# Hymba encoder layer on one core: the first group's last rows are multiplied on GpSimd and scaled on ScalarE instead of normed on VectorE

## The reference

```python
def rmsnorm(x, g):
    xf = x.astype(jnp.float32)
    y = xf * lax.rsqrt(jnp.mean(xf * xf, axis=-1, keepdims=True) + NORM_EPS)
    return (y * g.astype(jnp.float32)).astype(x.dtype)
...
    gu = jnp.einsum('bsd,dn->bsn', rmsnorm(x, ln_ffn_g), w_gate_up)
    g, up = gu[..., :D_FF], gu[..., D_FF:]
    return x + jnp.einsum('bsf,fd->bsd', jax.nn.silu(g) * up, w_down)
...
    return rmsnorm(x, final_norm_g)
```

## Time and profile before

| | |
|---|---|
| runs | 1387.62 us median of 3 (1386.29, 1387.62, 1387.71) |
| profiled execution | span of its instructions 1386.6 us; its device time is not listed apart from the runs |
| busy | TensorE 98%, VectorE 60%, ScalarE 49%, GpSimd 49% of the span |
| TensorE's granted clock, mean | 0.998 of full speed |
| the first group's norms on VectorE | 4 of 1.29 us (128x1024) |
| last instruction of ScalarE ends | 1382.84 us |
| last store issued | 1382.91 us |

### The profile page before, as it was taken

The page is one execution under the profiler, slowest core; times in us unless marked ns, Lnnn a source line. Parts: engine busy times, 40 slices in busy tenths (PEclk is TensorE's granted clock), DMA queues, the critical chain, the costliest instruction groups (busy, mean ns, idle before and its releaser), DMA issues.

```text
span 1386.6 us, 18049 instructions
## 1 busy us (share of the span) xinstructions
PE 1358.0 (98%) x6560; PEld 1139.1 (82%) x6560; DVE 831.7 (60%) x1133; ACT 672.8 (49%) x1252; POOL 677.4 (49%) x524
## 2 busy tenths in 40 slices
PE   8999999999999999999999899999999999999996
PEld 6977789888898778988887688888888888888885
DVE  3777647143457683642537885566566665488676
ACT  5577646445335874653547433233333233444446
POOL 4658858732445876694156755555555452000001
PEclk9999999999999999999999999999999999999999
DMA  8411154414322104352152242233322325973334
GB/s 282 157 31 39 31 183 146 156 33 137 105 61 84 46 9 160 118 188 76 62 193 80 69 155 89 99 113 108 115 96 102 114 85 194 327 252 114 100 94 149
DMA packets 101032, 164.63 MB, mean 119 GB/s; under 512 B 8785, under 2 KB 42961, under 8 KB 100945
## 3 DMA queue, kind: packets, MB, share of 16 engines
q1 hardware_dynamic: 100944, 163.49, 35.7%
HBM read 134.89 MB, written 28.57 MB: 118 GB/s over the span
## 4 chain that ended last, share of the span: by engine, by line
PE 91%; DVE 4%; ACT 2%; issue 1%; POOL 1%; DMA 1%; SPq 0%; ACTq 0%; DVEq 0%
PE ps L1994 28%; PE ps L1995 28%; PE ps L1996 28%; PE ps L2151 1%; PE ps L2179 1%; PE ps L2180 1%; PE ps L2183 1%; DVE h_lo_P L1387 1%; ACT junk L920 1%; POOL w_lo L764 1%; DVE x_res L1499 1%; PE ps L2367 1%; PE ps L2072 1%; ACT w_hi L898 0%; DMA a_raw<-a_mem 0%
## 5 line engine op out<-in xcount | busy, mean ns | idle before, releaser
L764 POOL TENSOR_TENSOR w_lo<-w_raw,w_hi 128x512 fp32r<-128x512 f32 (+2 forms) x236 | 306.8, 1318 | 223.1 <-ACT w_hi L898 222.8
L1994 PE MATMUL ps<-h_hi_P,w_hi 128*128 128x512 f32 x616 | 240.7, 391 | 4.9 <-issue 2.1
L1996 PE MATMUL ps<-h_hi_P,w_lo 128*128 128x512 f32 x616 | 239.7, 389 | 0.0
L1995 PE MATMUL ps<-h_lo_P,w_hi 128*128 128x512 f32 x616 | 239.7, 389 | 0.0
L898 ACT ACTIVATE w_hi<-w_raw 128x512 fp32r<-128x512 f32 (+2 forms) x236 | 141.3, 608 | 194.0 <-PE ps L1996 160.6
L764 POOL TENSOR_TENSOR w_lo<-w_sum,w_hi 128x512 fp32r<-128x512 f32 x88 | 118.8, 1354 | 115.7 <-ACT w_hi L898 115.7
L1994 PEld LDWEIGHTS ps<-h_hi_P,w_hi 128*128 128x128 f32 x616 | 115.6, 188 | 31.6 <-issue 4.1
L1994 PE MATMUL ps<-w_hi,act_hi 128*128 128x512 f32 (+2 forms) x384 | 141.0, 367 | 0.5 <-DVE z L1559 0.5
L1996 PE MATMUL ps<-w_hi,act_lo 128*128 128x512 f32 (+2 forms) x384 | 139.8, 364 | 0.0
L1995 PE MATMUL ps<-w_lo,act_hi 128*128 128x512 f32 (+2 forms) x384 | 139.8, 364 | 0.0
L1996 PEld LDWEIGHTS ps<-h_hi_P,w_lo 128*128 128x128 f32 x616 | 115.6, 188 | 24.1
(11 more groups left out here) (256 smaller groups left out, 3016.1 us busy)
## 6 DMA issues: line engine op xcount, KB each, us to landing
gu_raw<-in_w_gate_up SPq DMA_DIRECT2D x22, 1024.0 KB, 5.4
a_raw<-a_mem SPq DMA_DIRECT2D x77, 256.0 KB, 2.7
w_raw<-in_w_xkv SPq DMA_DIRECT2D x64, 256.0 KB, 3.3
a_mem<-down_sum SPq DMA_DIRECT2D x44, 256.0 KB, 2.6
wd<-in_w_down SPq DMA_DIRECT2D x44, 256.0 KB, 5.9
a_mem<-act_t SPq DMA_DIRECT2D x33, 256.0 KB, 2.1
w_raw<-in_w_out SPq DMA_DIRECT2D x32, 256.0 KB, 2.7
w_raw<-in_w_xq SPq DMA_DIRECT2D x32, 256.0 KB, 3.1
```

The source lines that it names most:

```text
L764: return nc.gpsimd.tensor_tensor(out, whole, hi.bitcast(F32), ALU.subtract)
L1994: nc.tensor.matmul(out, s_hi, m_hi, start=start, stop=False, skip_group_check=more)
L1995: nc.tensor.matmul(out, s_hi, m_lo, start=False, stop=False, skip_group_check=more)
L1996: return nc.tensor.matmul(out, s_lo, m_hi, start=False, stop=stop, skip_group_check=more)
```

## The change

The first group's final norm is divided over three engines. GpSimd multiplies each of its four row blocks by the weight vector, in place, after the block's square and after its own four multiplies of the second group. VectorE only makes the reciprocal. ScalarE applies the row factor with a Copy that has a scale per row: blocks 0 and 1 ahead of its loop over the second group, blocks 2 and 3 in the first two rounds of that loop; the second group's `last_rows` move back, to the third and fourth round and behind the loop. SyncE's stores now wait for ScalarE's `scaled_out` for all eight blocks, and for `out_ready` for the second group only. VectorE's wait for its own reciprocal goes for the first group. The order of the stores stays.

```diff
             for i in range(G * T):
-                sp.wait_ge(out_ready, i + 1)
                 if i >= T:
-                    sp.wait_ge(y22_ready, i - T + 1)
+                    sp.wait_ge(out_ready, i - T + 1)
+                sp.wait_ge(scaled_out, i + 1)
                 sp.dma_start(y[i // T, (i % T) * P:(i % T + 1) * P, :], x_res[:, i, :]).then_inc(out_sent, 16)
...
             for t in range(T):
                 pool.wait_ge(squares.sem, squares.at(G, T + t + 1))
                 o = x_res[:, T + t, BANK:D]
-                nc.gpsimd.tensor_tensor(o, o, y_gain[:, BANK:D], ALU.mult).then_inc(x22_gained, 1)
+                nc.gpsimd.tensor_tensor(o, o, y_gain[:, BANK:D], ALU.mult).then_inc(gained, 1)
+            for t in range(T):
+                pool.wait_ge(squares.sem, squares.at(G, 2 * T + t + 1))
+                nc.gpsimd.tensor_tensor(x_res[:, t, :], x_res[:, t, :], y_gain[:], ALU.mult).then_inc(gained, 1)
...
             def last_rows(t):
 
                 act.wait_ge(rstds.sem, rstds.at(G, 1 + T + t + 1))
-                act.wait_ge(x22_gained, t + 1)
+                act.wait_ge(gained, t + 1)
                 o = x_res[:, T + t, BANK:D]
-                nc.scalar.activation(o, o, ACT.Copy, scale=rstd[:, T + t:T + t + 1]).then_inc(y22_ready, 1)
+                nc.scalar.activation(o, o, ACT.Copy, scale=rstd[:, T + t:T + t + 1]).then_inc(scaled_out, 1)
+
+            def first_rows(t):
+
+                act.wait_ge(rstds.sem, rstds.at(G, 1 + t + 1))
+                act.wait_ge(gained, T + t + 1)
+                nc.scalar.activation(x_res[:, t, :], x_res[:, t, :], ACT.Copy,
+                                     scale=rstd[:, t:t + 1]).then_inc(scaled_out, 1)
+
+            first_rows(0)
+            first_rows(1)
 
             for t in range(T):
                 act.wait_ge(x21_done, t + 1)
...
-                if t >= 1:
-                    last_rows(t - 1)
+                if t < 2:
+                    first_rows(2 + t)
+                else:
+                    last_rows(t - 2)
+            last_rows(T - 2)
             last_rows(T - 1)
...
             def last_norm(t):
                 dve.wait_ge(stds.sem, stds.at(G, 1 + t + 1))
                 nc.vector.reciprocal(rstd[:, t:t + 1], std[:, t:t + 1]).then_inc(rstds.sem, 1)
-                dve.wait_ge(rstds.sem, rstds.at(G, 1 + t + 1))
-                if t < T:
-                    normed(x_res[:, t, :], x_res[:, t, :], t, y_gain[:]).then_inc(out_ready, 1)
-                else:
+                if t >= T:
+                    dve.wait_ge(rstds.sem, rstds.at(G, 1 + t + 1))
                     o = x_res[:, t, 0:BANK]
                     normed(o, o, t, y_gain[:, 0:BANK]).then_inc(out_ready, 1)
```

More of the change, by code:

```diff
@@ L435, in build @@
         x21_done = sem("x21_done")
-        x22_gained = sem("x22_gained")
+        gained = sem("gained")
         half_eps = sem("half_eps")
-        y22_ready = sem("y22_ready")
+        scaled_out = sem("scaled_out")
         out_ready = sem("out_ready")
```

## The result

The changed kernel takes **1389.38 us** (median of 20 runs, 1388.16 to 1390.76), the kernel before 1387.46 on the same chip (20 runs, 1385.93 to 1389.33): ratio **1.0016**, 95% interval 1.0010 to 1.0022, that is +1.9 us by the medians and +1.4 to +3.1 by the interval. Forecast were 1389.9 us and +2.3. The profiled execution of the changed kernel took 1388.16, the lowest of its 20 runs, and its span is 1386.4.

The account below looks back on a forecast made before the run. TensorE fills 91% of the span, so only the tail around its last matmuls was taken to count; two holds, ScalarE's longer chain and queued stores gave +2.3 on median 1387.62, 1389.9 us, range 1387.6 to 1391.0.

Parts of the forecast that it names:

- first subtraction of the last pair ends: VectorE's last two weight subtractions, needed by TensorE: the first, held by GpSimd's block 1, ends at 1370.99.
- second subtraction ends: VectorE's second of that pair, held by GpSimd's block 2, ends at 1373.80 instead of 1370.13; a 3.7 us wait.
- The multiply: GpSimd's 128x1024 multiply: 2.41 us when free, bounds 2.41 and 2.85.
- rival C: GpSimd's free 128x1024 multiply takes the whole 2.85 us, so +3.3, 1390.9 us; chance 0.15.
- The turns: VectorE's two-SBUF-operand subtractions and GpSimd's multiplies alternate one at a time; block 2 precedes the second subtraction, 3.7 us wait.
- Rival A: On VectorE's last pair the hold costs one step, not two, or none: +0.3, 1387.9 us; chance 0.20.
- Block 0's touch: GpSimd's block 0 multiply, ending 1366.75, costs VectorE's pair at 1366.43 some 0.2 us; TensorE has time for it.
- A pause of 3.1: TensorE, waiting for VectorE's held subtraction, pauses 3.1 us ahead of its last 24 matmuls.
- rival D: TensorE's clock falls to half in its pause; 24 slow matmuls add 5.4, end about +5, 1392.6 us; chance 0.04.
- ScalarE and the stores: ScalarE works without a gap from 1373.93 to 1384.51; the last three stores, 0.61 apart, queue and flow until 1387.99.
- rival B: As A, but the last three stores do not queue: -0.3, 1387.3 us; sign turns under 0.90 us a block; chance 0.03.

Follow-up runs that it names:

- e7_dummies2: Kernel before plus four GpSimd 128x1024 multiplies of two different tiles, one after each first-group square, result unread; 1393.80 us, ratio 1.0045.
- e3_dummies: Kernel before plus four GpSimd 128x1024 multiplies of the weight vector by itself, one after each first-group square, result unread; 1390.34 us, ratio 1.0023.
- e6_late2: The change, but GpSimd's multiplies of blocks 2 and 3 wait until VectorE's last pair of weight subtractions is done; 1387.11 us, ratio 1.0002 to before.
- e4_no_multiply: The change without GpSimd's four first-group multiplies and the wait for them, ScalarE's scalings kept; 1387.48 us, ratio 1.0003 to before.
- e9_mixed: Kernel before, GpSimd multiplying blocks 0 and 1 earlier, out of place; VectorE scales 0, ScalarE 1, block 3's norm after first last sum; 1385.07 us, ratio 0.9987.

## Why the prediction was right

In the prediction's frame t is the time less 1364.26; the trace of after gives:

| step | forecast, t | measured, t |
|---|---|---|
| first subtraction of the last pair ends | 1370.99: 6.73 | 1368.53: 6.73 |
| second subtraction ends | 1373.80: 9.54 | 1371.28: 9.48 |
| first scaling on ScalarE starts | 1373.93: 9.67 | 1371.39: 9.59 |
| GpSimd's block 3 ends | 1376.06: 11.80 | 1373.56: 11.76 |
| ScalarE ends | 1384.51: 20.25 | 1381.88: 20.08 |
| last store issued | 1384.58: 20.32 | 1381.95: 20.15 |
| transfers end | 1387.99: 23.73 | 1385.42: 23.62 |
| span ends | 1388.9: 24.64 | 1386.4: 24.60 |

- **The multiply.** 2.41 was taken from the row's 2.85 less a held part; 2.40 was measured. With it **rival C** falls, which had a free one take 2.85.
- **The turns.** That block 2 goes before the second subtraction was read from alternations of 128x512 operations; it holds for 128x1024 too (2.15 and 2.83, in the change and in e7_dummies2). The order was close: block 2 was issued 0.46 us ahead of the second subtraction, and in e3_dummies, where the subtraction was issued 0.05 ahead (1369.29 against 1369.34), it went first. All these rows fit order of issue as well as strict turns. Forecast were about 2.2 and 2.9. **Rival A**, one hold or none, would have given +0.3; e6_late2 and e4_no_multiply are its two forms and do give +0.34 and +0.35.
- **Block 0's touch.** The pair before the last was to lose some 0.2: its first subtraction takes 0.86 instead of 0.69.
- **TensorE.** A pause of 3.1 was forecast, 2.84 measured, and the granted clock stayed at 1.00 in every window of it and until the matmuls ended, with matmuls 0.23 apart on its far side: **rival D** did not come about in this execution. That was luck in part. In e7_dummies2 the clock did fall behind a pause of 2.82, so D's mechanism is real and its 0.04, resting on no pause having cost any so far, was low; its price was too high, 5.4 for 24 slow matmuls against the 1.6 measured there. Two of the 20 runs of the change have a mean granted clock of 0.995 and the longest spans, 1388.5 and 1389.0, the others 0.996 or 0.997 and 1386.4 to 1388.1; whether the clock fell in their pause is not shown.
- **ScalarE and the stores.** ScalarE has no wait after its first scaling, and the last three stores are 0.61 apart, as written. The transfers run at 401 to 418 GB/s in the full windows from 1383 to 1385, above 1.25 us a block, far from the 0.90 at which **rival B**'s sign would turn.

The sum was +2.3 and the tail shows +2.26: 0.35 for ScalarE and the stores (e4_no_multiply) and 1.9 for the holds. Between the medians it is +1.9, within the interval of +1.4 to +3.1. What the prediction did not say: of the 3.6 us that the two holds cost VectorE, 1.7 are slack of ScalarE, so the first is free on its own (e6_late2).

## What to carry to other kernels

A norm moved from VectorE to GpSimd is paid by whatever VectorE does with two SBUF operands at that moment, and they take turns: put GpSimd's reads where VectorE has no such instruction on the path, and count turns, not busy time. Before that, ask who is late next: the first hold's 1.5 us alone cost nothing, the two together, 3.6, cost 1.9, and in the kernel before, where VectorE's list has no slack, these two and a third cost 5.5. At the end of a kernel the order of the stores can be the bound: with the first store waiting for the slowest of the early blocks, 0.7 us of faster compute bought nothing until the order was changed.

## What was not expected of the hardware

- A GpSimd multiply of a 128x1024 fp32 tile by itself takes 1.89 us, that of two tiles 2.40 (e3_dummies, e7_dummies2).
- Once both have work queued, the two engines take turns, over four subtractions in a row in e9_mixed, beside multiplies of 128x512 and of 128x1024: a held 128x512 subtraction ends about 0.55 after the multiply's end. The held 128x1024 norm of e7_dummies2 ends 1.08 after it (1366.71 + 7.93 = 1374.64, and 1372.53 + 3.19 = 1375.72).
- Two pauses of TensorE of the same length, 2.84 and 2.82, ended with a granted clock of 1.00 in the change and of 0.50 in e7_dummies2.
